# Layer 0's attention in 32 pieces between the parts of the output projection, and the gate between the z parts

## The reference

```
o_a = window_attn_prompt(q, k, v, 1, slopes, sink)       # 4 blocks of 128 queries, each with its own and the previous 128 keys
g = y * silu(z); g = g * rsqrt(mean(g*g, per group of 512 features) + eps); y_ssm = g * norm_w
x = x + concat(o_a, y_ssm) @ w_out                       # 1024 + 2048 features in, 1024 out
```

## Time and profile before

| | |
|---|---|
| time, median of 3 runs | 2775.04 us (2771.96 to 2777.78) |
| time of the profiled execution | 2782.28 us |
| its span, first to last instruction | 2780.6 us |
| TensorE busy | 2455.1 us, 88% |
| VectorE, ScalarE, GpSimd busy | 1368.6, 725.5, 389.9 us |
| mean granted TensorE clock | 0.916 |

### The profile page before, as it was taken

The page is one execution under the profiler, slowest core; times in us unless marked ns, Lnnn a source line. Parts: engine busy times, 40 slices in busy tenths (PEclk is TensorE's granted clock), DMA queues, the critical chain, the costliest instruction groups (busy, mean ns, idle before and its releaser), DMA issues.

```text
span 2780.6 us, 43294 instructions
## 1 busy us (share of the span) xinstructions
PE 2455.1 (88%) x17994; PEld 2306.3 (83%) x17994; DVE 1368.6 (49%) x1874; ACT 725.5 (26%) x1466; POOL 389.9 (14%) x224
## 2 busy tenths in 40 slices
PE   5998998856559999999998998998899897899997
PEld 4986666645348999999997998998898797899997
DVE  4785776523247453344555354445535512533444
ACT  3332232212225222222312322322222221311221
POOL 1000332200000000000044134034214401000000
PEclk9998999967769999999999998999999956999999
DMA  4226766551232268777568477377556613578775
GB/s 143 64 86 217 257 235 234 188 209 56 35 127 93 85 227 272 256 256 262 205 218 265 156 229 234 107 231 224 185 162 232 219 62 106 197 257 271 265 262 183
DMA packets 295607, 526.07 MB, mean 189 GB/s; under 512 B 29184, under 2 KB 265072, under 8 KB 291488
## 3 DMA queue, kind: packets, MB, share of 16 engines
q1 hardware_dynamic: 284176, 331.71, 37.9%
q10 hardware_dynamic: 5888, 177.91, 17.5%
q0 software_dynamic: 5408, 14.56, 1.4%
HBM read 490.40 MB, written 210.91 MB: 252 GB/s over the span
## 4 chain that ended last, share of the span: by engine, by line
PE 68%; DVE 10%; DMA 10%; issue 4%; ACT 3%; POOL 3%; SPq 1%; DVEq 0%; ACTq 0%; POOLq 0%
PE gp L2134 34%; PE gp L2615 10%; DMA uk<-in_dil_k 6%; PE gp L2275 5%; PE mp L2573 4%; POOL uq L2719 3%; DVE cacc L1474 2%; PE mp L2505 2%; PE gp L2332 1%; DMA at_v<-tmp_v 1%; PE mp L2475 1%; DVE sc_t L1997 1%; PE mp L2230 1%; DMA tmp_stats_s<-sm_ms 1%; DVE hs_t L1598 1%
## 5 line engine op out<-in xcount | busy, mean ns | idle before, releaser
L2134 PE MATMUL gp<-a_hi,w_hi 128*128 128x272 f32 x1584 | 332.0, 291 | 12.0 <-DVE cin L1463 10.9
L2134 PE MATMUL gp<-a_lo,w_hi 128*128 128x272 f32 x1584 | 330.4, 290 | 0.0
L2134 PE MATMUL gp<-a_hi,w_lo 128*128 128x272 f32 x1584 | 329.0, 289 | 0.0
L2134 PE MATMUL gp<-b_hi,w_hi 128*128 128x272 f32 x1280 | 268.8, 291 | 31.7 <-DVE b_lo L1760 31.7
L2719 POOL TENSOR_TENSOR uq<-uq,uk 128x1024 f32<-128x1024 f32 x96 | 240.9, 2513 | 335.2 <-DMA uk<-in_dil_k 335.0
L2615 PE MATMUL gp<-a_hi,w_hi 128*128 128x272 f32 x1152 | 273.0, 319 | 0.1
L2134 PE MATMUL gp<-b_lo,w_hi 128*128 128x272 f32 x1280 | 267.1, 290 | 0.0
L2134 PE MATMUL gp<-b_hi,w_lo 128*128 128x272 f32 x1280 | 266.0, 290 | 0.0
L2134 PEld LDWEIGHTS gp<-a_hi,w_hi 128*128 128x128 f32 x1584 | 252.1, 190 | 14.9 <-DVE cin L1463 12.7
L2134 PEld LDWEIGHTS gp<-a_hi,w_lo 128*128 128x128 f32 x1584 | 251.5, 190 | 0.0
L2134 PEld LDWEIGHTS gp<-a_lo,w_hi 128*128 128x128 f32 x1584 | 249.8, 191 | 0.0
(11 more groups left out here) (348 smaller groups left out, 3981.4 us busy)
## 6 DMA issues: line engine op xcount, KB each, us to landing
out_dil_ks<-in_dil_k ACTq DMA_DIRECT2D x32, 2044.0 KB
out_dil_vs<-in_dil_v ACTq DMA_DIRECT2D x32, 2044.0 KB
uq<-tmp_rows SPq DMA_DIRECT2D x96, 512.0 KB, 4.8
w_raw<-in_odd_w_in SPq DMA_DIRECT2D x36, 1024.0 KB, 8.2
w_raw<-in_w_up SPq DMA_DIRECT2D x32, 1024.0 KB, 7.7
w_raw<-in_w_down SPq DMA_DIRECT2D x32, 1024.0 KB, 8.0
uk<-in_dil_k SPq DMA_DIRECT2D x64, 512.0 KB, 6.2
vr<-in_dil_v SPq DMA_DIRECT2D x64, 512.0 KB, 5.0
```

Source lines behind the costliest of these rows:

```text
L2134: m = nc.tensor.matmul(gp[:, c, h, 0:HALF], w[:, sl, k, c * P:(c + 1) * P], x[:, k, h * HALF:(h + 1) * HALF], start=n < 2, stop=n >= 46)
```

## The change

The order of the output groups becomes `out0_1`, `out0_2`, `out0_0`: gated features first, attention's last. A second table (`mix_events`) places work between the parts of 26 steps s: two without a chunk (parts 0 to 15), then the 24 chunks of the output projection.

- Attention is cut into 32 pieces p (half a head: two blocks of 128 queries). TensorE makes the scores at part 4p+2, turns the exps at 4p+8 and multiplies with the values at 4p+12. VectorE takes bias, maxima (now with the sink) at 4p+2 and the sum's reciprocal at 4p+5. ScalarE takes the exps of scores and sink at 4p+2 and copies the turned exps at 4p+8. The turning is no longer a transpose but a product with a diagonal of the reciprocals: GpSimd makes it from the identity, two 128 x 128 tiles a piece. So the output needs no factor afterwards, and the stores and loads of maxima, sums and factors are gone. Keys and values stay on chip for all heads, and q is loaded by the pair of heads.
- The samples go the same way, at parts 9, 17, 33 and 41, their factor multiplied into the exps on VectorE.
- The gate: the products with silu(z) of groups 0, 1 and 2 and their squares are made between the z parts, from parts 110, 152 and 172 on (load, silu 4 parts later, product 5, squares 7, sum of the four squares on VectorE 9), group 3 at parts 9 to 14 of the new steps. One ones-matmul per group adds over partitions, root on ScalarE, and `y_parts(g)` on VectorE (reciprocal, four products, four low parts) at parts 0, 8, 51 and 64; ScalarE makes the high parts.
- The sinks are brought onto all partitions once, early in the z parts, by a matmul that TensorE waits for at the end of z part 1.
- ScalarE's copies of caches by DMA change places: four window copies go into the z parts, eight copies of `dil1_v` from the z parts into the new steps. Constants of layer 1 are loaded by GpSimd's queue at the start of the MLP.

```diff
-    order += [("out0_0", 4), ("out0_1", 4), ("out0_2", 4), ("mlp0", 32)]
+    order += [("out0_1", 4), ("out0_2", 4), ("out0_0", 4), ("mlp0", 32)]
...
+Z_AT = ((16, 20, 17, 21), (17, 20, 21, 18), (18, 20, 21, 22), (19, 20, 21, 22))
+GATE_P = (110, 152, 172)
...
+    for g, part in enumerate((0, 8, 51, 64)):
+        at(dve, part, "y", g)
+        at(act, part, "y", g)
+    for r in range(4):
+        at(pe, 1, "keys", r)
+        at(act, 1, "keys", r)
+    at(pe, 1, "s0", 0)
+    at(act, 1, "s0", 0)
+    at(act, 9, "silu", 3)
+    at(dve, 10, "gate", 3)
+    at(act, 12, "square", 3)
+    at(dve, 14, "gsum", 3)
+    for part, what in ((25, "root"), (28, "root_s")):
+        at(pe, part, what, 3)
+        at(act, part, what, 3)
+    for p in range(32):
+        s = 4 * p + 2
+        for d, q, what in ((pe, s, "scores"), (dve, s, "scores"), (act, s, "exps"), (dve, s + 3, "sums"), (pe, s + 6, "turn"),
+                           (act, s + 6, "turn"), (pe, s + 10, "values")):
+            at(d, q, what, p)
+        if p % 4 == 3:
+            at(act, s + 10, "out", p // 4)
+            at(dve, s + 10, "out", p // 4)
+    for hb in range(4):
+        s = 9 + 8 * hb if hb < 2 else 17 + 8 * hb
+        for d, q, what in ((pe, s, "s_scores"), (dve, s, "s_scores"), (act, s, "s_exps"), (dve, s + 2, "s_sums"),
+                           (pe, s + 5, "s_turn"), (act, s + 5, "s_turn")):
+            at(d, q, what, hb)
+    for d in (pe, dve):
+        at(d, 49, "s_out", 0)
+    for d in (act, dve):
+        at(d, 82, "s_split", 0)
+    for C in range(2, 8):
+        at(sp, 16 * C - 16, "q", C)
...
+            def load_z(g):
+
+                sp.wait_ge(y_done, (10, 15, 15, 20)[g])
+                if g:
+                    sp.wait_ge(gate_sum, g)
+                sp.wait_ge(st_done[0], 16 * (6 + 2 * g))
+                sp.wait_ge(st_done[1], 16 * (6 + 2 * g))
+                for j in range(4):
+                    sp.dma_start(xbc[:, Z_AT[g][j]], scratch["z0"][4 * g + j]).then_inc(z_in, 16)
+
...
+            def exps(p):
+
+                n0 = P if p % 2 == 0 else 2 * P
+                flat = at_e[:, p % 2].rearrange("p a b -> p (a b)")
+                act.wait_ge(nm_done, p + 1)
+                for j, e in enumerate((flat[:, 0:n0], flat[:, n0:n0 + 2 * P])):
+                    nc.scalar.activation(e, e, ACT.Exp, bias=at_m[:, p, j:j + 1], accum_out=at_n[:, p, j:j + 1])
...
+                        if 8 * z + part == at0 + 5:
+                            gates(g)
+                        if 8 * z + part == at0 + 9:
+                            gate_sums(g)
...
+            def y_parts(g):
+
+                root = xbc[:, 16 + g]
+                dve.wait_ge(root_done, g + 1)
+                dve.wait_ge(root_s_done, 1 + g // 3)
...
+                    wait(dve, y_hi_done, C - 1)
+                    wait(dve, y_rdy, C - 1)
+                    nc.vector.scalar_tensor_tensor(out=xw[:, C % 2], in0=xbc[:, C], scalar=c_at["ssm_norm"][:, C:C + 1],
+                                                   in1=root, op0=ALU.mult, op1=ALU.mult).then_inc(y_val, 1)
+                    if j:
+                        y_low(C - 1)
+                y_low(4 * g + 3)
...
+            def y_low(C):
+
+                dve.wait_ge(y_val, C + 1)
+                dve.wait_ge(y_hi_done, C + 1)
+                if C == 8:
...
+            def scores_out(p):
+
+                h = p // 2
+                flat = at_e[:, p % 2].rearrange("p a b -> p (a b)")
+                slope = at_slope[:, h:h + 1]
+                if p == 0:
+                    dve.wait_ge(atd_in, 64)
+                dve.wait_ge(s_mm, p + 1)
+                wait(dve, t_mm, p - 1)
+                if p % 2 == 0:
+                    st.link(nc.vector.scalar_tensor_tensor(out=flat[:, 0:384], in0=at_d[:].rearrange("p a b -> p (a b)"), scalar=slope,
+                                                           in1=mp[:, 0, 0:384], op0=ALU.mult, op1=ALU.add))
+                    nc.vector.tensor_reduce(at_m[:, p, 0:1], flat[:, 0:P], AX.X, ALU.max, negate=True)
+                    st.link(nc.vector.tensor_reduce(at_m[:, p, 1:2], flat[:, P:384], AX.X, ALU.max, negate=True))
+                else:
+                    e = flat.rearrange("p (t k) -> p t k", t=2)
+                    d = at_d[:, 1:3].rearrange("p (o a) b -> p o (a b)", o=1).to_broadcast([P, 2, 2 * P])
+                    st.link(nc.vector.scalar_tensor_tensor(out=e, in0=d, scalar=slope,
+                                                           in1=mp[:, 0].rearrange("p (t k) -> p t k", t=2), op0=ALU.mult, op1=ALU.add))
+                    st.link(nc.vector.tensor_reduce(at_m[:, p], e, AX.X, ALU.max, negate=True))
+                nc.vector.tensor_scalar(at_m[:, p], at_m[:, p], nsink[:, h:h + 1], None, ALU.min).then_inc(nm_done, 1)
+
+            def sums_of(p):
+
...
+            for s in range(N_MIX + 1):
+                d = s - N_PRE - 1
+                if d >= 0:
+                    X = 2 * G0["out0_1"] + d + 1
+                    if d in (0, 5, 6):
+                        dve.wait_ge(x_in, 16 * (4 if d >= 5 else 3))
+                    dve.wait_ge(mm_done, X)
+                    add_x("out0", 0, d % 8)
+                    if d >= 16:
...
+            def turn(p):
+
+                pe.wait_ge(diag_done, p + 1)
+                wait(pe, t_done, p)
+                if p == 0:
+                    pe.wait_ge(root_done, 3)
+                for j in range(4 if p % 2 else 3):
+                    tile = j // 2 if p % 2 else (j + 1) // 2
+                    m = nc.tensor.matmul(mp[:, 1, j * P:(j + 1) * P], at_e[:, p % 2, j], at_f[:, p % 2, tile], start=True, stop=True)
+                m.then_inc(t_mm, 1)
+
...
+                for part in range(8):
+                    if d >= 0:
+                        if d % 8 == 0:
+                            if d < 16:
+                                pe.wait_ge(y_rdy, d + part + 1)
+                            else:
+                                pe.wait_ge(b_ready, part + 1)
+                                pe.wait_ge(so_rdy, 1)
+                        hi = xbc_hi[:, 8 * (d // 8) + part]
+                        lo = y_lo[:, 8 * (d // 8) + part] if d < 16 else o_lo[:, part]
+                        for j, (w, x) in enumerate(((w_hi, hi), (w_lo, hi), (w_hi, lo))):
+                            for h in range(2):
+                                m = nc.tensor.matmul(gp[:, c, h, 0:HALF], w[:, G % 2, part, c * P:(c + 1) * P],
+                                                     x[:, h * HALF:(h + 1) * HALF], start=part == 0 and j == 0,
+                                                     stop=part == 7 and j == 2)
+                        if part == 7:
...
+            for p in range(32):
+                pool.wait_ge(f_done, p + 1)
+                wait(pool, t_mm, p - 1)
+                for t in range(2):
+                    z = nc.gpsimd.tensor_scalar(at_f[:, p % 2, t], ident[:], at_n[:, p, t:t + 1], None, ALU.mult)
+                z.then_inc(diag_done, 1)
```

More of the change, by code:

```diff
@@ L692, in _ @@
             for z in range(N_PROJ):
[L693 removed]
+                if z % 2 == 0 and z < N_PROJ:
                     n = z // 2 + 2
@@ L819, in _ @@
[L819 to L831 removed]
+            sp.wait_ge(h_out, 16 * NG_SSM)
@@ L1096, in attention @@
-            def attention(call):
-                def body(c2, last):
-                    for cc in range(2):
-                        for half in range(2):
-                            exps(call, c2, cc, half)
-                            if half == 0:
-                                if isinstance(c2, int) and c2 == 0 and cc == 0:
-                                    continue
-                                o_out(call, c2 * 2 + (cc - 1), 1 - cc)
-                turns(act, 4, body, peel_first=2 if call == 0 else 1)
-                o_out(call, 7, 1)
```

1049 lines of the change are left out of this document (463 added, 586 removed).

## The result

| | before | after |
|---|---|---|
| time, median (8 runs each, same chip) | 2777.90 us | 2755.45 us (2750.28 to 2762.93) |
| profiled execution | 2782.28 us | 2762.51 us |
| mean granted clock | 0.916 | 0.921 |

The ratio is 0.9915 (95% interval 0.989 to 0.9939). The change is faster, but by 22 us and not by 111.5, and the time lies outside my range. The stages show where the rest went. Each mark is the start of a matmul that opens a stage: the first root's ones-product, the first output matmul, and the sums of squares. In before the z parts end with the drain of their last chunk, 563.54 us in the earlier trace rows; that drain starts at 594.6 us in after.

The account below looks back on a forecast made before the run. TensorE, busy 88% of the span, was taken as the bound. Its block would take 13 + 33 + 231 + 27 = 304 us instead of 415.5, a gain of 111.5, giving 2663.5 us; range 2625 to 2710.

Parts of the forecast that it names:

- 231 of work: TensorE's own work in the block: output projection 144.2 us, 16 heads 81 us, samples and last root 6 us.
- 27 of stalls: TensorE's stalls among the output parts: `y_parts` blocks, weight split, start, clock and table changes; 27 us, bounds 8 and 60.
- the first step: Two steps without a chunk before the first output part: 5 + 19 + 3 + 6 = 33 us, bounds 24 and 42.
- the weight split: Start of each output group: ScalarE's and VectorE's split delays the turn about 0.7 us, eleven times, 8 us.
- rival 4: Stalls among the parts keep TensorE's clock at its lower level; slower than before, 2883 us; chance 0.02.
- The blocks among the parts: `y_parts(2)` at part 51 and `y_parts(3)` at 64 delay VectorE's sum that a turn awaits: 4 and 8 us.
- The diagonals: GpSimd's two tiles per attention piece, taken as 0.4 us, within a chain with 3.8 us to spare.
- The z parts: Added time in the z parts from gate sums, group 2's steps and sinks: 13 us together, bounds 3 and 30.
- The gate itself: Gate work of groups 0 to 2 inside the z parts: 2.2, 2.2 and 7.6 us.
- rival 2: GpSimd and VectorE hold each other up, `w_lo` steps delaying the diagonals: 25 us, 2689 us; chance 0.08.
- The table loads: ScalarE's table switches cost only the 1.28 us load; the skill's added drain would make three switches 4 us longer.
- The tail: Everything after the block (sum of squares, MLP) stays as it is.

Follow-up runs that it names:

- all_mended: Changed kernel with y_spread, keys_first, gate_later and pad_after's edits, and the window copy moved from z = 16 to z = 20: 2671.28 us, ratio 0.9593.
- y_spread: Changed kernel with reciprocal and scaling (`y_parts`) of groups 1 to 3 given out one tile at a time instead of in one block: 2741.38 us, ratio 0.9847.
- keys_first: Changed kernel with ScalarE's four copies of turned keys ahead of its `y` copies of group 0: 2748.64 us, ratio 0.9852.
- gates_small: Changed kernel with the gate of groups 0 to 2 touching only 8 columns of each tile instead of 544: 2747.13 us.
- gsum_later: Changed kernel with the gate's three additions of squares given to VectorE three parts later: 2751.57 us, ratio 0.9852.
- nops_after: Changed kernel with 128 empty TensorE instructions before layer 1's MLP, dropped at build, so a repeat of it: 2755.55 us, ratio 0.991.
- pad_after: Changed kernel with 64 real TensorE instructions ahead of the last statistics matmul, before layer 1's MLP loop: 2716.98 us, ratio 0.9736.
- pad32_after: Changed kernel with 32 counting TensorE instructions ahead of layer 1's MLP loop: 2732.13 us, ratio 0.9797.
- unrolled: Changed kernel with TensorE's loop of layer 1's MLP written out four times, without a back edge: 2724.04 us, ratio 0.9777.
- pad_before_4: Kernel before with 1085 counting TensorE instructions ahead of the last MLP loop, placing it where the changed kernel has it: 2946.89 us.
- mended_early: all_mended with the third group's z loads and steps 6 parts earlier and the window copy at z = 14 instead of 20: 2673.26 us, ratio 0.9608.
- pad_before: Kernel before with 61 real TensorE instructions ahead of its last statistics matmul: 2789.83 us, ratio 1.0019.
- gate_later: Changed kernel with silu, products, squares and sums of groups 0 to 2 at 7, 8, 10 and 12 parts: 2752.2 us, ratio 0.9885.

## Why the prediction was wrong, step by step

- **From the first to the last output matmul: the sum near, by luck in part.** Forecast 258 us, 231 of work and 27 of stalls; measured 264.6. The work was set too low. In all_mended TensorE is busy for 243.6 us over the same 1749 matmuls at a clock of 0.99, and part of the 231 us is already done in the first step. The stalls were set too high: after's 264.6 us less these 243.6 leave 21 us, of which 16.9 are idle time (12.1 for `at_pt`, 4.7 for the diagonals) and the rest is the lower clock. For the weight split, 8 us in my sum, no wait stands in the trace. So the two errors cancel. Which matmuls take longer between the parts than my rows said isn't separated here. The clock's collapse of rival 4 didn't come: 0.96.
- **The blocks among the parts: the right place, the wrong engine.** 4 us forecast for `y_parts(2)`, 3.14 measured at 715.86; 8 forecast for `y_parts(3)`, 8.93 measured; and y_spread shows that these blocks were the cause. But I let the turn wait for the sum behind the block on VectorE. In the trace the wait ends with ScalarE's copy of an earlier turn, which stands behind the block's four roundings, and I had not looked at ScalarE's order there. My number for the second block was wrong by my own rule too: by 4p+8 no turn stands at part 66, the next one behind part 64 is at 68, which gives 9.5 + 1.2 - 5.5 = 5 us and not 8. So 8 against 8.93 is luck.
- **The diagonals: undersized.** They were forecast too short (0.614 us each on GpSimd, not 0.4), which costs little: 5.9 us of waits in nine.
- **The first step: 33 forecast, 47.3 measured.** The same step failed here: ScalarE's order. I had the keys' copies between the fourth and the fifth rounded tile and charged 3 us on VectorE. That is where they are. But on TensorE's side the cached scores and everything behind them wait for these copies, and they stand behind all of `y_parts(0)`: 8.61 us. keys_first alone takes the step to 37.5 us. The second block, `y_parts(1)`, was also a TensorE wait of 6.67 us for the first piece; y_spread takes the step to 40.8 us, and both edits take it to 31.2.
- **The z parts: 13 forecast, 31.3 measured.** The step that failed is the one that isn't in my sum. The diff moves four window copies into the z parts, and I priced only the other copies, those of `dil1_v`, beside the output weights. The copy at z = 16 cost 10.7 us by holding SyncE. The gate itself was near: 14.4 us by gates_small, 12 in my sum, and near by group too. Its make-up is less sure, since the sums, 5.4 us of my 12, gave back only 1.6 us when gsum_later moved them. The sinks I had at 1 us. The store of `hs_t` ahead of the first gate step stands at 374.38 us in after and at 371.30 in before, 3.1 us apart; but it stands at 372.01 and 372.15 us in the two other kernels of before's kind and at 372.17 in nops_after, so this is not told from the spread of executions. 31.3 - 14.4 - 10.7 = 6.2 us are left for the sinks and for what I haven't found, if the parts add up.
- **The port of rival 2 was real, in another place, and free.** It stretched the gate's additions and hardly the diagonals (38.6 us for 64), and gsum_later shows no price beyond the spread. The Trainium skill, page "SBUF — State Buffer", section "Terms", has the loser of the shared port pair fully blocked for the whole instruction. The trace agrees: of the three additions at 437.67 two took 2.47 and 2.74 us, about as long as the two GpSimd instructions beside them (2.35 and 2.82), and the third, behind them, 0.73.
- **The table loads: sized rightly.** In after's first step:
```profile
595.98 1.28 ACT L1097 ACT_TABLE_LOAD   x1 [14.27 <-PE mp L2304]
597.27 1.85 ACT L1097 ACTIVATE xbc<-mp,eps_col 128x512 f32<-128x512 f32 x3
```
  The first root starts 0.01 us after the load's end. The Trainium skill, page "ScalarE: Activation LUTs", section "What ACT_TABLE_LOAD costs", adds some 1.38 us of drain to a load; these rows don't show it either. In the same step the load at 637.36 us starts 0.02 us behind the silu before it, and the exp starts 0.01 us behind its end.
- **The tail: 0 forecast, 51.7 measured.** 36.3 us are layer 1's MLP. That its refetched loop costs them is shown by pad_after, pad32_after and unrolled (390.8, 389.8 and 389.8 us for 426.4); what makes it refetch at one place and not at another stays open. I took "not edited" for "not changed". The edit made TensorE's program longer ahead of the loop, and no step of mine asked what that moves.
- **Layer 1, 14.3 us: left open.** Its work is the same in all 17 profiled executions without pad_before_4, whose 1085 instructions stand in this stage (the 61 or 64 of other kernels lengthen it by at most about 1 us, by the wait at its end). It took from 999.5 to 1030.2 us in them: three of before's kind 999.5, 1002.5 and 1003.3, fourteen of after's kind 1002.4 to 1030.2. After, then mended_early, the second shortest of its kind:
```profile
1302.20:2319.00 1016.80, 926.13 (x6648) 887.65 (x6648) 453.22 (x736) 260.99 (x662) 282.72 (x146) 0.88 0.56 181
```
```profile
1262.50:2265.30 1002.80, 909.45 (x6648) 871.18 (x6649) 453.54 (x736) 260.62 (x662) 281.38 (x146) 0.90 0.56 183
```
  The matmuls are as many, and 17 us more busy at a clock of 0.88 for 0.90. All three of before's kind are among the five shortest of the 17, which speaks for a tilt by the change and not for chance alone; by which path it would come no run shows.

Together: 18.3 (z parts) + 14.3 (first step) + 6.6 (parts) + 1.1 + 14.3 + 36.3 = 90.9 us, the gap between the 111.5 us forecast and the 19.8 us by which the two profiled executions differ, to within 0.8, most of which stands behind the last sum of squares. all_mended lies 84 us below after's median and 8 us above the number that I had forecast; as a ratio to the kernel before 0.9593, where 2663.5 to 2775.04 is 0.9598. That is no proof of my sum: by stage all_mended has 18.7, 31.2 and 249.6 us where I had 13, 33 and 258, and it lacks the blocks for which I had charged 12 us. What held is the idea, to fill the waits of the block with other work. What failed is that I priced each edit on the engine that runs it, and not what stands behind it in the orders of ScalarE and SyncE, nor the code behind it.

## What to carry to other kernels

Price every instruction that a diff moves by the queue that it lands in: a large copy just ahead of a load holds the engine that issues the load, and all that stands behind it. Where a helper is a block of 10 us on one engine, look up who in another engine's order waits behind it, and hand it out in pieces on both engines. A stage's time can be right while its terms are not, so compare busy time and idle time each by itself. When a stage that nobody edited gets slower, look at its loops' turns and at the instruction queue first; a few instructions more ahead of the loop, or no loop, show whether the loop is the cause.

## What the runs showed of the hardware

- The instructions of a TensorE loop (some 100 KB, 769 matmuls a turn) were either fetched once for four turns (6 packets of 16 KB) or again each turn (34 packets), and then TensorE waited 9.9 to 10.4 us at each of the three turns. In between lay pad_before, with 16 packets and waits of 3.4 and 3.3 us. Straight code fetched 25 packets over the same work without a wait.
- The same instruction place, by count, was bad in one program and harmless in another (pad_before_4).
- The issue of one 2 MB load took 19.21 us on SyncE beside a 4 MB copy of another queue, 1.16 us without it.
- VectorE's additions of two tiles in SBUF took 6.01 us for three beside GpSimd's work, 2.24 us without it.
- In gate_later TensorE was idle for 5.9 us less over the same 873 matmuls, in more waits, and busy for 6.6 us longer at a mean clock of 0.84 instead of 0.87; the z parts ended when they had in after.
